# Joining the two maps of differential attention ahead of the transposes, and issuing the first tile's output projection within the last attention steps

## The chip, the cores and the metric

One core of a Trainium2 chip runs the whole program. The metric is device time in microseconds (us) of one execution; lower is better. Five engines work side by side and meet through semaphores: TensorE (PE, matmuls), VectorE (DVE), ScalarE (ACT), GpSimd (POOL) and SyncE (SP), which issues the weight loads. Each engine takes its own instructions strictly in the order of the program.

## The reference

Two transformer layers over 256 tokens of width 1024, all in float32. Layer 0: swiglu, post-norm, a sparse attention (NSA), post-norm, swiglu, post-norm; its result also gives shared keys and values. Layer 1: swiglu, post-norm, differential attention, post-norm, swiglu, post-norm. The change is in the differential attention, eight heads with two maps each:

```python
lam = exp(sum(lq1 * lk1)) - exp(sum(lq2 * lk2)) + lambda_init
a = attn_map(q1b, k1) - lam * attn_map(q2b, k2)      # causal softmax maps, head dim 64
o = einsum('bhqk,bkhe->bqhe', a, v)                  # value dim 128
o = rms_norm(o, subln_g) * (1.0 - lambda_init)
return o.reshape(B, S, D_MODEL) @ w_out
```

## The kernel before, in words

**Weights.** A weight matrix passes in units of 128x2048 values through four slots of `raw`, `w_hi` and `w_lo`. SP loads a unit once the unit four before it is split. Splitting means: ACT copies `raw` to a rounded `w_hi` (L575), DVE subtracts for `w_lo` (L781); in the attentions POOL does both in quarters (L502, L503). A product is then three matmuls, hi by hi, hi by lo and lo by hi (`three`, L1193 to L1195). `unit_used` frees a slot when PE has finished a unit for token tile 1. Tokens go in two tiles of 128. Each stage (`STAGES`) fills `acc` banks 0 and 1 for tile 0, then 2 and 3 for tile 1; a norm of DVE (L822 to L835) reads them, with a root by POOL (L480, L481), and its gain and bias come by a DMA of POOL (`load_norm`, L475) into `norm_gb`, whose space the probabilities share until the last of them is transposed.

**Differential queries.** Stage `diff_q` has four units. While PE runs tile 1 of it, it also transposes the rotated keys (L1252) and swaps their halves (L1438); ACT copies the even parts of four (L589), DVE the odd ones (L814), from two banks of `trb` in turn. Each turned part needs the part two before it to be copied. DVE evicts the queries (L1102), POOL rotates them (L488 to L491), ACT and DVE split them (`split_beside`, L603, L808), and PE turns them, those of tile 0 before the loop, those of tile 1 within its steps 2 to 5 (`LATE_PARTS`).

**The loop.** `DIFF_JOBS` has 12 jobs: tile 0 has four jobs of two heads (maps of 128 keys), tile 1 eight jobs of one head (maps of 256 keys). A job fills one bank of 512 columns. `DIFF_TURNS` groups them: turn 0 is jobs 0 and 1, turn 1 jobs 2 and 3, turn 2 jobs 4 to 7, turn 3 jobs 8 to 11; a turn fills one 512-wide output per map. `job_steps` gives 15 steps. At step i, each engine in its own order:
- PE: scores of job i (L1375, and the mask L1377) into the bank i modulo 3 of three, after the exponentials of job i-3; transposes of the four probability blocks of job i-2; late query parts; value products of job i-3 (L1396), map 0 into `acc[:, 2]`, map 1 into `acc[:, 3]`.
- ACT: copy of the turned blocks of job i-2 (L589), late query parts, exponentials of job i, with their row sums (L664).
- DVE: negated maximum of job i (L930); the pieces of a finished turn: `diff_read` (L1134 to L1138: reciprocals of the sums, times lambda, both outputs scaled out of PSUM), one step later `diff_subtract` (L1151 to L1154: difference, square, reduce, scale and epsilon), then POOL's power -1/2 (L557) and `diff_norm` (L1161, L1162).
- At steps 10 and 11 (`TILE0_DONE`) PE turns the two halves of the finished tile 0 (`("x", "diff_o", 0)`), ACT and DVE write their high and low parts (L583, L791).
- POOL, beside the loop, splits units 0 and 1 of the output projection, then the powers, with unit 2 after the second; the norm's gain and bias are loaded after the third power. Unit 3 is split by ACT and DVE behind the loop.

**The projection.** `out_stage` waits for the last exponential, runs the four units for tile 0 (16 products of three matmuls), with the turns of tile 1 ahead of its last unit (`turn_o`, waits for the last norm), then tile 1. DVE's norm of tile 0 starts when `tile0_full` says so (L822); behind it DVE splits the first units of the next swiglu, `ffn3`.

## Time and profile before

| what | us |
|---|---|
| runs of the kernel: median, lowest, highest of 3 | 1071.84, 1071.44, 1075.18 |
| the profiled execution, its own time | 1070.39 |
| its span, first to last instruction | 1068.3 |
| PE, DVE, ACT, POOL busy in the span | 1033.2, 596.3, 460.7, 125.1 |
| mean granted clock of TensorE | 0.997 |

The durations below are of the one profiled execution, its times counted from the start of its span. A granted clock of 1.00 is TensorE's full 2.4 GHz. Successive instructions of an engine overlap a little, so that the distance from start to start is shorter than the duration shown; where work is summed up, that distance counts.

### The profile page before, as it was taken

The page shows a single profiled execution, that of the slowest core. Times are in us where ns is not written, and L with a number is a line of the kernel's source. Part 1 is how long each engine was busy: PE and PEld are TensorE (multiplying, and loading weights), DVE is VectorE, ACT ScalarE, POOL GpSimd, SP SyncE. Part 2 cuts the span into 40 slices and gives each one's busy share as a digit, 9 for nine tenths or more (in the row PEclk, how much of TensorE's full clock was granted, in tenths as well). Part 3 has the DMA queues.
Part 4 walks back from the last instruction along what each step waited for, and adds up shares of the span by engine and source line. Part 5 has one row for each costly group of instructions (what it writes and reads, how often), then busy time and mean ns, then how long its engine had stood idle before and what let it go on. Part 6 is the DMA issues. An engine that isn't in the chain of part 4 may idle for free.

```text
span 1068.3 us, 13273 instructions
## 1 busy us (share of the span) xinstructions
PE 1033.2 (97%) x5334; PEld 868.8 (81%) x5334; DVE 596.3 (56%) x543; ACT 460.7 (43%) x568; POOL 125.1 (12%) x157
## 2 busy tenths in 40 slices
PE   7999999999999999999999999999997899999997
PEld 6888888889898788898878888888876778888885
DVE  4455543854755754462575544554666884455444
ACT  4555432333773454452434334433436444454430
POOL 1000000232911100000012000000017510000001
...
DMA packets 78652, 178.51 MB, mean 167 GB/s; under 512 B 2992, under 2 KB 12352, under 8 KB 78608
## 3 DMA queue, kind: packets, MB, share of 16 engines
...
q14 instruction: 11, 0.09, 0.0%
...
## 4 chain that ended last, share of the span: by engine, by line
PE 82%; DVE 13%; POOL 3%; ACT 1%; DMA 1%; issue 1%; SPq 0%; POOLq 0%; DVEq 0%; ACTq 0%
PE acc L1193 24%; PE acc L1195 24%; PE acc L1194 24%; DVE w_lo L781 4%; PE trb L1252 4%; PE acc L1396 2%; POOL rstd L480 1%; DVE stats L827 1%; DVE x L835 1%; DVE y L822 1%; PE acc L1375 1%; DMA raw<-ffn_w_gate 1%; DVE neg_max L930 1%; DVE xt_lo L791 1%; PE aux L1445 1%
## 5 line engine op out<-in xcount | busy, mean ns | idle before, releaser
L781 DVE TENSOR_TENSOR w_lo<-raw,w_hi 128x2048 fp32r<-128x2048 f32 (+1 forms) x153 | 348.7, 2283 | 217.4 <-ACT w_hi L575 217.4
L575 ACT ACTIVATE w_hi<-raw 128x2048 fp32r<-128x2048 f32 (+1 forms) x153 | 291.7, 1908 | 259.0 <-PE acc L1195 252.1
L1193 PE MATMUL acc<-w_hi,xt_hi 128*128 128x512 f32 (+1 forms) x992 | 378.8, 382 | 6.0 <-DVE w_lo L781 4.6
L1195 PE MATMUL acc<-w_hi,xt_lo 128*128 128x512 f32 (+1 forms) x992 | 371.9, 375 | 0.0
L1194 PE MATMUL acc<-w_lo,xt_hi 128*128 128x512 f32 (+1 forms) x992 | 371.4, 374 | 0.0
L1193 PEld LDWEIGHTS acc<-w_hi,xt_hi 128*128 128x128 f32 x992 | 186.9, 188 | 41.0 <-DVE w_lo L781 6.5
L1195 PEld LDWEIGHTS acc<-w_hi,xt_lo 128*128 128x128 f32 x992 | 186.7, 188 | 34.2
L1194 PEld LDWEIGHTS acc<-w_lo,xt_hi 128*128 128x128 f32 x992 | 187.1, 189 | 31.4
L1193 PE MATMUL acc<-w_hi,ht_hi 128*128 128x512 f32 x352 | 139.4, 396 | 0.0
L1195 PE MATMUL acc<-w_hi,ht_lo 128*128 128x512 f32 x352 | 138.9, 395 | 0.0
L1194 PE MATMUL acc<-w_lo,ht_hi 128*128 128x512 f32 x352 | 138.9, 395 | 0.0
L480 POOL TENSOR_SCALAR rstd<-mean_var 128x1 f32<-128x1 f32 x12 | 15.2, 1268 | 796.0 <-DVE mean_var L829 787.9
L1195 PEld LDWEIGHTS acc<-w_hi,ht_lo 128*128 128x128 f32 x352 | 66.3, 188 | 15.5
L1193 PEld LDWEIGHTS acc<-w_hi,ht_hi 128*128 128x128 f32 x352 | 66.3, 188 | 15.0
L1194 PEld LDWEIGHTS acc<-w_lo,ht_hi 128*128 128x128 f32 x352 | 66.3, 188 | 15.0
L619 ACT ACTIVATE ht_hi<-trb 128x512 f32 (+2 forms) x48 | 26.7, 556 | 109.1 <-PE trb L1252 109.1
L851 DVE TENSOR_TENSOR ht_lo<-trb,ht_hi 128x512 f32 (+2 forms) x48 | 30.5, 642 | 72.7 <-ACT ht_hi L619 72.7
L615 ACT ACTIVATE y<-acc 128x512 f32<-128x512 f32 (+1 forms) x48 | 27.0, 563 | 73.3 <-PE acc L1195 73.3
L846 DVE SCALAR_TENSOR_TENSOR y<-y,acc 128x512 f32<-128x512 f32 (+1 forms) x48 | 30.7, 639 | 45.4 <-ACT y L615 45.4
L583 ACT ACTIVATE xt_hi<-trb 128x512 fp32r<-128x512 f32 x32 | 17.7, 596 | 64.4 <-PE trb L1252 64.4
L503 POOL TENSOR_TENSOR w_lo<-raw,w_hi 128x512 fp32r<-128x512 f32 x28 | 37.8, 1349 | 2.2
L1252 PE MATMUL trb<-id_r,y 128*128 128x128 f32 x200 | 30.5, 272 | 3.8 <-POOL y L525 1.7
...
## 6 DMA issues: line engine op xcount, KB each, us to landing
...
```

What stands on the lines that cost most here:

```text
L480: link(pool.tensor_scalar(rstd[:, tok, 0:1], mean_var[:, tok, 1:2], EPS, None, ALU.add))
L503: ins = pool.tensor_tensor(w_lo[:, slot, part], raw[:, slot, part], hi.bitcast(F32), ALU.subtract)
L575: act.activation(w_hi[:, slot, 0:k * c], raw[:, slot, 0:k * c], ACT.Copy).then_inc(hi_ready, 1)
L615: act.activation(sil[:, tok, 0:c], acc[:, 2 * tok, 0:c], ACT.Silu).then_inc(silu_done, 1)
L619: act.activation(ht_hi[:, bass.ds(4 * g, k), tok * P:(tok + 1) * P], trb[:, bank, 0:k * P].rearrange("p (k c) -> p k c", c=P), ACT.Copy).t ...
L781: dve.tensor_tensor(w_lo[:, slot, 0:k * c], raw[:, slot, 0:k * c], w_hi[:, slot, 0:k * c].bitcast(F32), ALU.subtract).then_inc(lo_ready, 1)
L846: dve.scalar_tensor_tensor(h_nat[:, tok, 0:c], sil[:, tok, 0:c], 0.5, acc[:, 2 * tok + 1, 0:c], ALU.mult, ALU.mult).then_inc(acc_free, 1)
L851: dve.tensor_tensor(ht_lo[:, bass.ds(4 * g, k), tok * P:(tok + 1) * P], trb[:, bank, 0:k * P].rearrange("p (k c) -> p k c", c=P), ht_hi[:, ...
L1193: pe.matmul(out_ap, s_hi, hi, start=first, stop=False)
L1194: pe.matmul(out_ap, s_hi, lo, start=False, stop=False)
L1195: return pe.matmul(out_ap, s_lo, hi, start=False, stop=last)
L1252: ins = pe.transpose(trb[:, bank, j * P:(j + 1) * P], b, ident)
```

## The change

- **Order of a job.** When a job's exponentials are done, DVE joins its two maps in SBUF (`join_maps`): a reciprocal of the second sums, a small product with the first sums and minus lambda, and for each head one `scalar_tensor_tensor` over the map (first + share * second). PE then transposes two blocks in place of four and multiplies two in place of four; the output of a turn lies in one bank, turns alternating between `acc[:, 2]` and `acc[:, 3]`. The division by the first sum is left out, and the norm's epsilon is scaled by the sum's square instead.
- **Norm.** The squares with their sums go to ACT, from PSUM (`squares_of`), two small operations to DVE (`diff_sums`), the power stays with POOL, and `diff_norm` reads PSUM in four pieces; it runs at fixed steps 6, 8 and 12. `diff_read` and `diff_subtract` go. Turn 2 and 3 wait, before their first product, for the norm that read their bank.
- **Order on the engines.** ACT runs the exponentials of a step before its copies. DVE copies the first two late query parts, and splits the last queries in step 0, behind the first maximum. The last key copy goes ahead of the eviction of the second queries.
- **Projection.** Tile 0 of it is cut into eight pieces of six matmuls (`diff_out_piece`), issued in steps 10 (one), 11 (one), 12 (two), 13 (one), two behind the loop, one behind the turn of tile 1. Since they use `acc` banks 0 and 1, scores 9 to 11 use the two `aux` banks (`diff_bank`). Halves of tile 0 are turned at steps 7 and 9.
- **Splits and loads.** Units 0 and 1 of the projection are split by ACT and DVE between the key copies, units 2 and 3 by POOL from step 0 on, unit 3 in halves between the powers. `load_norm(4)` comes after the fourth power.

The diff, cut to its core:

```diff
 
-TILE0_DONE = {"nsa": (14, 15), "diff": (10, 11)}
+TILE0_DONE = {"nsa": (14, 15), "diff": (7, 9)}
+
+DIFF_NORM_STEP = {0: 6, 1: 8, 2: 12}
+
+DIFF_OUT_STEPS = {10: (0,), 11: (1,), 12: (2, 3), 13: (4,)}
 
 LATE_PARTS = {"nsa": {6: (0,), 9: (1,), 11: (2,), 13: (3,)}, "diff": {2: (0,), 3: (2,), 4: (1,), 5: (3,)}}
...
         score_bank = [acc[:, 0], acc[:, 1], aux[:, 0]]
+        diff_bank = [score_bank[i % 3] for i in range(9)] + [aux[:, 1], aux[:, 0], aux[:, 1]]
...
-            split_units(UNIT_OF["diff_out"], UNIT_OF["diff_out"] + 2)
-            for k in range(len(DIFF_TURNS)):
+            n = UNIT_OF["diff_out"] + 2
+
+            def diff_root(k):
                 pool.wait_ge(rms_ready, k + 1)
-                pool.tensor_tensor(rms[:, 1, k, :], rms[:, 0, k, :], half_pow[:], ALU.pow).then_inc(rms_pow, 1)
-                if k == 1:
-                    split_units(UNIT_OF["diff_out"] + 2, UNIT_OF["diff_out"] + 3)
-                if k == len(DIFF_TURNS) - 2:
-                    load_norm(4)
+                pool.tensor_tensor(rms[:, 2, k, :], rms[:, 1, k, :], half_pow[:], ALU.pow).then_inc(rms_pow, 1)
+
+            pool.wait_ge(beside_ready, 8)
+            pool.wait_ge(lo_ready, n)
+            split_unit(n)
+            diff_root(0)
+            split_unit(n + 1, range(2))
+            diff_root(1)
+            split_unit(n + 1, range(2, 4))
+            diff_root(2)
+            diff_root(3)
+            load_norm(4)
...
+
+            def copy_joined(j):
+                t = TURN_OF["p", "diff", j]
+                act.wait_ge(tr_full, t + 1)
+                act.activation(turned_probs[:, j % 2, 0:2 * P], trb[:, t % 2, 0:2 * P], ACT.Copy).then_inc(
+                    tr_free[t % 2], 1)
+
+            def squares_of(turn):
+
+                act.wait_ge(turn_full, len(NSA_TURNS) + turn + 1)
+                for k in range(4):
+                    ins = act.activation(branch[0][:, k * DIFF_V:(k + 1) * DIFF_V],
+                                         acc[:, 2 + turn % 2, k * DIFF_V:(k + 1) * DIFF_V], ACT.Square,
+                                         accum_out=rms[:, 0, turn, k:k + 1])
+                ins.then_inc(squares_summed, 1)
+
+            def split_parts(n, parts):
+
+                slot, (k, c) = n % SLOTS, unit_shape(n)
+                act.wait_ge(raw_in[slot], 16 * (n // SLOTS + 1))
+                act.wait_ge(unit_used, n - SLOTS + 1)
+                for q in parts:
+                    part = slice(q * k * c // 4, (q + 1) * k * c // 4)
+                    ins = act.activation(w_hi[:, slot, part], raw[:, slot, part], ACT.Copy)
+                if q == 3:
+                    ins.then_inc(hi_ready, 1)
 
...
             act.activation(lam[:, 0:2], lam[:, 0:2], ACT.Exp).then_inc(lam_exp, 1)
+            split_units(n0 + 4, n0 + 5)
 
             for part in (0, 2):
                 copy_heads(("kr", "diff"), 0, part, dks[:, 0])
...
+                split_parts(n0 + 5, (part, part + 1))
             for tok in range(TOKS):
                 for part in (0, 2):
...
-                if tr:
-                    copy_p("diff", i - 2)
-                for part in LATE_PARTS["diff"].get(i, ()):
-                    copy_heads(("qr", "diff"), 1, part, dqs)
                 if sc:
                     exps("diff", DIFF_JOBS, i, len(NSA_JOBS))
+                if tr:
+                    copy_joined(i - 2)
+                if i > 3:
+                    for part in LATE_PARTS["diff"].get(i, ()):
+                        copy_heads(("qr", "diff"), 1, part, dqs)
+                if pv >= 0 and DIFF_JOBS[pv][3]:
+                    squares_of(DIFF_JOBS[pv][0])
                 if i in TILE0_DONE["diff"]:
                     x_high("diff_o", 0, [TILE0_DONE["diff"].index(i)])
-            act.wait_ge(lo_ready, n0 + 7)
-            split_units(n0 + 7, n0 + 8)
             x_high("diff_o", 1)
...
+            split_parts(n0 + 4, (0, 1))
+            copy_heads("kr", 0, 1, dks[:, 0])
+            split_parts(n0 + 4, (2, 3))
+            copy_heads("kr", 0, 3, dks[:, 0])
             split_beside(6)
-            for part in (1, 3):
-                copy_heads("kr", 1, part, dks[:, 0])
-            for part in (1, 3):
-                copy_heads("ks", 0, part, dks[:, 1])
+            copy_heads("kr", 1, 1, dks[:, 0])
+            copy_heads("kr", 1, 3, dks[:, 0])
+            split_parts(n0 + 5, (0,))
+            copy_heads("ks", 0, 1, dks[:, 1])
+            split_parts(n0 + 5, (1,))
+            copy_heads("ks", 0, 3, dks[:, 1])
             copy_heads("ks", 1, 1, dks[:, 1])
+            copy_heads("ks", 1, 3, dks[:, 1])
             diff_queries_out(1)
-            copy_heads("ks", 1, 3, dks[:, 1])
             for part in (1, 3):
                 copy_heads("qr", 0, part, dqs)
-            split_beside(7)
-
-            def diff_read(turn):
+            split_parts(n0 + 5, (2, 3))
...
+            def join_maps(i):
+
+                _, tok, heads, _ = DIFF_JOBS[i]
+                width = P * (tok + 1)
+                hs = slice(heads[0], heads[-1] + 1)
+                dve.wait_ge(exp_done, len(NSA_JOBS) + i + 1)
+                link(dve.reciprocal(share[:, 1, hs], sums[:, tok, 1, hs]))
+                link(dve.scalar_tensor_tensor(share[:, 0, hs], sums[:, tok, 0, hs], lam[:, 3:4], share[:, 1, hs],
+                                              ALU.mult, ALU.mult))
+                for k, h in enumerate(heads):
+                    first = probs[:, i % 3, 2 * k * width:(2 * k + 1) * width]
+                    second = probs[:, i % 3][:, (2 * k + 1) * width:(2 * k + 2) * width]
+                    ins = dve.scalar_tensor_tensor(first, second, share[:, 0, h:h + 1], first, ALU.mult, ALU.add)
+                ins.then_inc(maps_joined, 1)
...
+                first_sums = sums[:, tok, 0, 4 * g:4 * g + 4]
+                link(dve.scalar_tensor_tensor(rms[:, 1, turn, :], first_sums, EPS, first_sums, ALU.mult, ALU.mult))
+                dve.wait_ge(squares_summed, turn + 1)
+                dve.scalar_tensor_tensor(rms[:, 1, turn, :], rms[:, 0, turn, :], 1.0 / DIFF_V, rms[:, 1, turn, :],
+                                         ALU.mult, ALU.add).then_inc(rms_ready, 1)
...
+                o, to = acc[:, 2 + turn % 2], dq[:, tok, g * 512:(g + 1) * 512]
                 dve.wait_ge(rms_pow, turn + 1)
...
+                for k in range(4):
+                    at = slice(k * DIFF_V, (k + 1) * DIFF_V)
+                    ins = dve.scalar_tensor_tensor(to[:, at], o[:, at], rms[:, 2, turn, k:k + 1], sub_g[:], ALU.mult,
+                                                   ALU.mult)
+                ins.then_inc(turn_mixed, 1)
+
             for i, sc, tr, pv in job_steps(DIFF_JOBS):
                 if sc:
-                    maxima(DIFF_JOBS, i, len(NSA_JOBS))
-                for turn in range(last):
-                    if ends_turn(DIFF_JOBS, pv - 1, turn):
-                        diff_subtract(turn)
-                    if turn < 2 and ends_turn(DIFF_JOBS, pv - norm_lag[turn], turn):
+                    maxima(DIFF_JOBS, i, len(NSA_JOBS), diff_bank[i])
+                if i == 0:
+                    split_beside(7)
+                if i and i - 1 < len(DIFF_JOBS):
+                    join_maps(i - 1)
+                if i <= 3:
+                    for part in LATE_PARTS["diff"].get(i, ()):
+                        copy_heads("qr", 1, part, dqs)
+                for turn in range(len(DIFF_TURNS) - 1):
+                    if i == DIFF_NORM_STEP[turn]:
                         diff_norm(turn)
                 if pv >= 0 and DIFF_JOBS[pv][3]:
-                    diff_read(DIFF_JOBS[pv][0])
+                    diff_sums(DIFF_JOBS[pv][0])
                 if i in TILE0_DONE["diff"]:
                     x_low("diff_o", 0, [TILE0_DONE["diff"].index(i)])
-            diff_subtract(last)
-            diff_norm(last - 1)
-            diff_norm(last)
-            split_units(n0 + 7, n0 + 8)
+            diff_norm(len(DIFF_TURNS) - 1)
             x_low("diff_o", 1)
             out_stage("diff_out")
             ffn_stage("ffn3", lambda: x_low("diff_out", 1))
...
+                    pe.wait_ge(acc_free, e + 1)
+                elif DIFF_JOBS[j - 1][3] and turn_no >= 2:
+                    pe.wait_ge(turn_mixed, len(NSA_TURNS) + turn_no - 1)
...
+                    for kb in range(tok + 1):
+                        ins = pe.matmul(acc[:, 2 + turn_no % 2, (h % 4) * DIFF_V:(h % 4 + 1) * DIFF_V],
+                                        turned_probs[:, j % 2, k * P:(k + 1) * P],
+                                        v_b[:, kb, h * DIFF_V:(h + 1) * DIFF_V], start=(kb == 0), stop=(kb == tok))
+                        k += 1
+                if last:
+                    ins.then_inc(turn_full, 1)
+
+            def diff_out_piece(kt):
+
+                n = UNIT_OF["diff_out"] + kt // 2
+                if kt == 0:
+                    pe.wait_ge(exp_done, len(NSA_JOBS) + 8)
+                if kt % 4 == 0:
+                    copied("x", "diff_o", 0, kt // 4)
+                pe.wait_ge(lo_ready, n + 1)
+                for c in range(2):
+                    cols = slice(c * 512, (c + 1) * 512)
+                    ins = three(acc[:, c], xt_hi[:, kt, 0:P], xt_lo[:, kt, 0:P], weights(w_hi, n)[:, kt % 2, cols],
+                                weights(w_lo, n)[:, kt % 2, cols], kt == 0, kt == KT - 1)
+                if kt == KT - 1:
+                    finish(0, ins)
...
+                    pe.wait_ge(acc_free, e)
                     for tok, part in parts:
                         copied("ks", "diff", tok, part)
                 if sc:
-                    scores(DIFF_JOBS, i, base, lambda h, m: dqs[:, 8 * m + h],
+                    if i >= 3:
+                        pe.wait_ge(exp_done, len(NSA_JOBS) + i - 1 - (i < 10))
+                    scores(DIFF_JOBS, i, diff_bank[i], lambda h, m: dqs[:, 8 * m + h],
                            lambda h, m, part: dks[:, part, 8 * m + h])
+                for kt in DIFF_OUT_STEPS.get(i, ()):
+                    diff_out_piece(kt)
                 if tr:
-                    turn_p("diff", i - 2, base)
+                    pe.wait_ge(maps_joined, i - 1)
+                    _, tok, heads, _ = DIFF_JOBS[i - 2]
+                    turn(("p", "diff", i - 2), [probs[:, (i - 2) % 3, j * P:(j + 1) * P]
+                                                for j in ((0, 1) if tok else (0, 2))])
                 for part in LATE_PARTS["diff"].get(i, ()):
                     turn_heads(("qr", "diff"), 1, part, 7)
                 if pv >= 0:
-                    values("diff", DIFF_JOBS, pv,
-                           lambda h, m, kb: v_b[:, kb, h * DIFF_V:(h + 1) * DIFF_V], DIFF_V, diff_first, 4)
+                    diff_values(pv)
                 if i in TILE0_DONE["diff"]:
                     half = TILE0_DONE["diff"].index(i)
                     pe.wait_ge(turn_mixed, len(NSA_TURNS) + half + 1)
                     turn_wide(("x", "diff_o", 0), dq[:, 0, :], [half])
-            out_stage("diff_out", "diff_o")
+            for kt in (5, 6):
+                diff_out_piece(kt)
+            pe.wait_ge(turn_mixed, len(NSA_TURNS) + len(DIFF_TURNS))
+            turn_wide(("x", "diff_o", 1), dq[:, 1, :])
+            diff_out_piece(7)
+            group(1, FILL_OF["diff_out", 0, 1], UNIT_OF["diff_out"], range(4), rows_unit(xt_hi, xt_lo, KT),
+                  {3: lambda: turn_x("diff_out", 0)}, ("x", "diff_o", 1))
             ffn_stage("ffn3", lambda: turn_x("diff_out", 1), ("x", "diff_out"), False)
```

## Rows read from the trace of the kernel before

**Rows 1.** Page: chain that ended last, shares by engine; two costly groups of instructions.
```profile
PE 82%; DVE 13%; POOL 3%; ACT 1%; DMA 1%; issue 1%; SPq 0%; POOLq 0%; DVEq 0%; ACTq 0%
...
L781 DVE TENSOR_TENSOR w_lo<-raw,w_hi 128x2048 fp32r<-128x2048 f32 (+1 forms) x153 | 348.7, 2283 | 217.4 <-ACT w_hi L575 217.4
L575 ACT ACTIVATE w_hi<-raw 128x2048 fp32r<-128x2048 f32 (+1 forms) x153 | 291.7, 1908 | 259.0 <-PE acc L1195 252.1
```
**Rows 2.** Table by stage: length; PE, PEld, DVE, ACT, POOL busy (count); clock, DMA, GB/s.
```profile
788.60:803.20 14.60, 14.60 (x78) 11.13 (x77) 5.97 (x8) 5.73 (x9) 1.96 (x4) 1.00 0.00 1
817.20:843.20 26.00, 20.10 (x172) 18.62 (x172) 24.40 (x39) 16.10 (x53) 18.23 (x18) 1.00 0.27 86
842.00:843.00 1.00, 0.00 (x0) 0.00 (x0) 0.96 (x3) 0.00 (x0) 0.37 (x1) 1.00 0.82 121
843.20:846.70 3.50, 3.41 (x20) 3.44 (x21) 0.28 (x2) 2.40 (x2) 1.63 (x3) 0.62 0.87 331
```
**Rows 3.** Timeline of PE: start us, duration us, line, operation, count, [idle before <- releaser].
```profile
805.35 1.06 PE L1252 MATMUL trb<-id_r,y 128*128 128x128 f32 x8 [1.57 <-DVE dks L814]
...
807.40 0.41 PE L1375 MATMUL acc<-dks,dqs 128*128 128x128 f32 x2
...
830.89 0.48 PE L1375 MATMUL acc<-dks,dqs 128*128 128x256 f32 x2
...
831.65 0.61 PE L1252 MATMUL trb<-id_r,norm_gb 128*128 128x128 f32 x4
832.09 1.06 PE L1396 MATMUL acc<-v_b,y 128*128 128x128 f32 x8
832.91 0.48 PE L1375 MATMUL acc<-dks,dqs 128*128 128x256 f32 x2
```
**Rows 4.** Timeline of DVE, same columns, 784 to 862 us.
```profile
784.09 0.28 DVE L1094 TENSOR_TENSOR y<-lam_in 128x128 f32<-128x128 f32 x1
...
784.61 2.35 DVE L808 TENSOR_TENSOR dqs<-k_nat,dqs 128x1024 fp32r<-128x1024 f32 x2
...
808.40 1.88 DVE L808 TENSOR_TENSOR xt_lo<-k_nat,xt_lo 128x1024 fp32r<-128x1024 f32 x1 [0.19 <-ACT xt_lo L603]
...
819.04 0.98 DVE L1135 TENSOR_SCALAR share<-share,lam 128x4 f32<-128x4 f32 x1
...
821.27 0.68 DVE L930 TENSOR_REDUCE neg_max<-aux 128x2 f32<-128x512 f32 x1
821.87 1.15 DVE L1151 TENSOR_TENSOR k_nat<-k_nat,y 128x512 f32<-128x512 f32 x1
...
829.14 0.69 DVE L1152 TENSOR_TENSOR y<-k_nat 128x512 f32<-128x512 f32 x1
...
839.99 1.65 DVE L1152 TENSOR_TENSOR y<-k_nat 128x512 f32<-128x512 f32 x1
...
843.29 0.23 DVE L1135 TENSOR_SCALAR share<-share,lam 128x4 f32<-128x4 f32 x1
...
859.17 1.22 DVE L822 SCALAR_TENSOR_TENSOR y<-x,acc 128x1024 f32<-128x1024 f32 x1 [1.25 <-PE acc L1195]
...
861.99 1.28 DVE L832 SCALAR_TENSOR_TENSOR y<-y,mean_var,norm_gb 128x1024 f32<-128x1024 f32 x1
```
**Rows 5.** Timeline of POOL in the attention, same columns.
```profile
818.73 1.27 POOL L503 TENSOR_TENSOR w_lo<-raw,w_hi 128x512 fp32r<-128x512 f32 x1
...
825.71 1.03 POOL L557 TENSOR_TENSOR rms<-rms,half_pow 128x4 f32<-128x4 f32 x1 [1.55 <-DVE rms L1154]
...
844.49 0.66 POOL L475 DMA_DIRECT2D norm_gb<-norm_gain  x1 [0.85 <-PE trb L1252]
```
**Rows 6.** Timeline of ACT: one exponential of a first-tile job.
```profile
811.27 0.36 ACT L664 ACTIVATE norm_gb<-acc,neg_max 128x128 f32<-128x128 f32 x1
```
**Rows 7.** Chain of waits, one product of the output projection (start us, us).
```profile
854.84 0.23 PE acc L1193
```
**Rows 8.** DMA issues, 840 to 866 us: KB each, median us to landing.
```profile
norm_gb<-norm_bias POOLq DMA_DIRECT2D x1, 512.0 KB, 4.7
```

123 lines of the change are left out of this document (54 added, 69 removed).

## The prediction

> **What bounds the kernel now.** I read the chain that ended last first: TensorE (PE) holds 82% of it and VectorE (DVE) 13% [rows 1]. The weight products that fill most of the span are not touched, so the question is which stretch of DVE the change reaches. The table by stage answers: from 817.2 to 843.2 us, inside the differential attention, DVE is busy 24.4 of 26.0 us and PE 20.1 of 26.0; in the stretch before it, 788.6 to 803.2, PE is full and DVE and ScalarE (ACT) are busy 6.0 and 5.7 of 14.6 us [rows 2]. Then the order of PE: it idles 1.57 us at 805.35 for a key copy on DVE, starts the scores of step 0 at 807.40 and those of step 10 at 832.91 [rows 3]; the queue of VectorE takes up the first projected tile (L822) at 859.17 [rows 4]. From there on the two kernels do the same work, and DVE is again what the chain runs through, so the price of the change is the shift of that 859.17. Three pieces: up to step 0, steps 0 to 9, and step 10 to the end of tile 0.
>
> **The lock.** DVE's operations with all operands in SBUF wait for a running GpSimd (POOL) operation: the 128x4 tensor_scalar takes 0.98 us at 819.04 and 0.23 at 843.29; a 128x512 tensor_tensor takes 1.15 and 1.65 beside POOL, 0.69 without (829.14); the 128x1024 one 1.88 beside it and 1.2 (2.35 for two) without [rows 4]. POOL's operation that ran at 819.04 had started at 818.73 and took 1.27 [rows 5]: DVE resumed when it ended. Over the 11 such operations that began while POOL split weights (the first at 808.40, the last at 839.99), the excess adds to 5.1 us, 0.45 each. Maxima, copies and norms that read PSUM show no excess. The change gives DVE many small operations of the waiting kind.
>
> **Piece 1, up to step 0: minus 1.5 us, then 0.5 back.** The last key copy now precedes the 1.2 us eviction of the queries, so the 1.57 us idle ahead of the second query turn goes [rows 3]; scores 0 start near 805.9. The splits of output units 0 and 1 leave POOL: twice 1.9 us more on ACT, one and a half times 2.2 us (2.28 less the overlap) more on DVE [rows 1], inside 788.6 to 803.2, where each has over 8 us idle [rows 2]; hidden, and if they were not, PE's turns of the keys would be late by what sticks out. The second half of unit 1 (1.1 us) lies on DVE's path, at 806.6, and meets POOL's rotation: 0.5 us more, which delays the rotated queries and so the first exponentials. POOL starts unit 2 only after the query split of step 0, which so takes 1.2 us in place of 1.88 [rows 4].
>
> **Piece 2, steps 0 to 9.** Removed from DVE for a turn: two scaled reads, subtract, square, reduce, two norm operations, some 5.2 us without waits (seven 512-wide passes at 0.6 to 0.7 and three small ones). Added: a join for every job. Its two 128x256 or 128x128 halves are nearest to the 0.28 us of a 128x128 tensor_tensor [rows 4]; pipelined, with 1.07 ns an element from there to 0.69 at 512, 0.2 each for two heads or 0.37 for one. With the reciprocal (0.22) and the small product of sums (0.26, nearest to the 0.23 of the tensor_scalar), a join is 0.86 us. PE needs, before scores 10, the norm of turn 1 in DVE's step 8. DVE's account from 806.6 to there: 9 maxima at 0.60 (821.27 to 821.87 [rows 4]) 5.4; 8 joins 6.9; half unit 1.1; query split 1.2; two late copies 1.2; two norms of four 128-wide pieces (0.2 each as above, and the hand-over) 1.7; two sets of small sums 0.9; one low part 0.6: 19.0, with hand-overs 19.6. POOL splits units 2 and 3 beside it, so joins 0, 1, 2 (three waiting operations each) and 4 to 7 (two each), plus one small sum, wait: 18 x 0.45 = 8.1, and 0.5 from piece 1. Waits on others: the squares of turn 0 hold DVE 2.4 us, since ACT must first finish the exponentials and copies of that step and then four squares, priced as the 0.36 of a 128-wide exponential [rows 6], 1.4 in all; the high part of the turned tile holds it 0.5. Behind the waiting instruction stands the next step's maximum, for which ACT waits, then the join, then PE's turn. 19.6 + 8.6 + 2.9 = 31.1: DVE is through at 837.7, and scores 10 start at 837.9 where they stood at 832.91: **5.0 us later**. PE loses half its transposes and value products here (four transposes 0.44, 831.65 to 832.09, and values 0.82, to 832.91, per job [rows 3]; 0.63 us a job saved) but it is not the one that is late. In front of scores 4, for example, stand three joins and two copies, where ACT copied before.
>
> **Piece 3, from scores 10 to L822 of tile 0.** Before: 859.17 - 832.91 = 26.3. Now PE has work throughout: two score groups at 0.76 (830.89 to 831.65 [rows 3]) 1.5; seven pieces of the projection, each 6 products at 0.23 [rows 7], 9.7; four turns at 0.22 0.9; five value groups at 0.41 2.0: 14.1, so 852.0. DVE and ACT keep up (join 11 is due some 2 us before PE wants it). The last turn's values end two pieces (2.8) earlier, at 849.2; squares 1.4, small sums 0.45, POOL's power 1.03 [rows 5], norm 0.85 and hand-overs 0.3 make 853.2: PE idles 1.2 there. Eight transposes 0.9, piece seven 1.4, hand-over 0.2: 855.7. **17.8 in place of 26.3, minus 8.5.** Unit 3's split and DVE's 2.2 us for it leave this stretch; they were off the path. The load of the norm's gain moves behind the last power: issued near 852.1, it takes 0.66 to issue [rows 5] and 4.7 to land [rows 8], so 857.5; L832 wants it 2.8 us after L822 (859.17 to 861.99 [rows 4]), 858.5. It is hidden with 1 us to spare; beyond that each microsecond would be lost in full. The tighter ring of two banks for scores 10 and 11 waits for exponentials that are over: nothing.
>
> **Sum:** 5.0 - 8.5 = **-3.5 us**. The profiled execution is 1070.39 (span 1068.3 and 2.1 around it), so 1066.9 there; the median of the runs is 1.45 above it, so 1068.3.
>
> Bounds: the lock costs from 0 (joins that fall between POOL's operations; sum -11.6, 1060.2) to a whole 1.27 us operation [rows 5] for most of the 18 (up to 23, +11). I take 0.45, the mean of the same kind of operation beside the same POOL work. The joins themselves may be 0.1 to 0.3 off each, 1 to 3 us.
> The rows show a 128x1024 scalar_tensor_tensor with two SBUF tensors at 1.28 us (861.99) beside 1.2 for a tensor_tensor of that size [rows 4]: no halved rate.
> The Trainium skill, Vector Engine (DVE) Microarchitecture Reference, Points that are easy to get wrong, says such an operation with two sources that are not bf16 runs at half throughput; the twelve joins would then cost about 3 us more by an estimate from its factor, the sum -0.5 and the time 1071.3; the row of this case speaks against it, and it gets no chance of its own.
>
> **Rivals.**
> *Lock cheap (0.25).* The joins meet POOL half as often: the pattern maximum, reciprocal, join gives POOL's operation 0.8 us to end. For: the reciprocal and the maximum take no lock. Against: after each join the waiting POOL operation starts at once. Price: 4 of the 8.1 us back, 1064.3.
> *The clock (0.15).* TensorE was granted 1.00 at 842 to 843, where it did nothing, and 0.62 on the mean of the next stretch, 843.2 to 846.7 [rows 2], its level of 1.2 GHz in place of 2.4 for three quarters of it: of 2.7 us at half speed 1.3 are lost, or 1.5 with the edge. The new loop leaves PE idle some 3 us at step 2 and 2 to 3 us at steps 4 and 8, with less work between. Two such falls where PE is next late cost 3.0: 1071.3. Against: from 817.2 to 843.2, with 5.9 us of idle, the clock was 1.00 throughout [rows 2].
> The Trainium skill, TensorE: Matmul & The Clock Gate, HAM oscillation, warns of just this, idle gaps that bring back the low clock each time; the row from 843.2 agrees, the stretch before it does not.
> *Slower (0.08).* Place: between stt and join, and between the two joins of a job, where a POOL operation that queued meanwhile goes first. Then the 18 operations wait 0.95 us each, 9 more: 1077.3. It decides against the change from 0.64 us a wait (3.5/18 + 0.45). Against: the trace's mean of 0.45.
> *It doesn't do what it says (0.07).* The pieces are issued in steps 10 to 13, but PE has no idle time to fill there and pushes maxima 11 and join 11 back; the last norm comes later by as much: about no change, 1071.8.
> *Forecast (0.45):* 1066 to 1070.5.
>
> **Numbers.** What a measurement of this kernel can tell from no change is about 0.5%, 5.4 us. Faster by more: the lock rival (0.25) and a fifth of the forecast (0.09), 0.34. Slower by more: 0.08 and a little of the clock, 0.09. The rest 0.57. The range reaches down over most of the cheap lock (1062) and up over the clock and no change (1074.5); it leaves out the slow rival and the extreme of the cheap one.
>
> **What would show it.** Right: scores 0 near 806; scores 10 near 838; joins of 0.25 to 0.4 us alone and 0.8 to 1.5 beside POOL; PE full from step 10 until one idle of about 1 us before the last turn; L822 at 855 to 856; no table load before the squares. Wrong: scores 10 before 834 (lock overpriced) or after 841 (underpriced); granted clock 0.5 in the loop more than once; L832 idle on the gain's load; DVE not the releaser of PE's waits in steps 2 to 9.

## The result and the profile after

| kernel | runs | median, us | lowest to highest, us | ratio to the kernel before, 95% interval |
|---|---|---|---|---|
| before, beside it | 8 | 1073.98 | 1071.22 to 1075.56 | |
| changed | 8 | 1064.88 | 1063.88 to 1069.02 | 0.9933 [0.9914, 0.9952] |
| changed, once more (e0_after) | 12 | 1068.05 | 1063.75 to 1069.81 | 0.9951 [0.9934, 0.9968] |

The ratios weigh all runs, and so differ from the ratios of the two medians (which are 9.1 and 3.3 us apart); in the second comparison the kernel before has a median of 1071.36 us. The change makes the kernel faster, by 0.67% (7.2 us, from 5.2 to 9.2) in the first comparison and by 0.49% (5.3 us, from 3.4 to 7.1) in the second. The forecast was 3.5 us and a time of 1068.3. The range held; the forecast size was half to two thirds of what came. The likeliest verdict, no difference beyond 0.5%, lies at the edge of the first interval and in the middle of the second. The profiled execution took 1065.26 us (span 1063.3, granted clock 0.992), beside 1070.39 and 1068.3 of before.

The page has the same chain: PE first, then DVE, whose small share fell by a point [rows 1].

```profile
PE 81%; DVE 12%; POOL 2%; ACT 2%; issue 1%; DMA 1%; SPq 0%; POOLq 0%; DVEq 0%; ACTq 0%
```

Table by stage, columns as in [rows 2]: the key stage, scores 0 to scores 10, scores 10 to the norm of tile 0, then three pieces of the loop.

```profile
788.00:802.50 14.50, 14.02 (x74) 10.25 (x73) 9.65 (x15) 9.28 (x14) 1.73 (x4) 1.00 0.22 73
805.90:836.60 30.70, 21.98 (x153) 19.60 (x153) 26.03 (x57) 17.54 (x79) 18.95 (x21) 0.83 0.23 74
836.60:854.90 18.30, 17.23 (x99) 13.94 (x97) 9.05 (x30) 8.39 (x36) 3.15 (x4) 1.00 0.27 86
...
811.00:815.00 4.00, 2.20 (x11) 2.20 (x11) 3.93 (x7) 2.68 (x16) 3.84 (x5) 0.52 0.41 158
815.00:819.00 4.00, 3.40 (x19) 2.99 (x18) 3.93 (x8) 1.92 (x10) 2.74 (x3) 0.63 0.03 4
819.00:823.00 4.00, 3.31 (x26) 2.85 (x27) 1.76 (x7) 2.15 (x11) 0.00 (x0) 1.00 0.77 259
```

The splits of output units 0 and 1 fit beside the keys, but not for nothing: PE is busy 14.0 of 14.5 us there, where it was busy all of the time before. In the loop DVE is busy 26.0 of 30.7 us, and from scores 10 on PE 17.2 of 18.3. The clock is 0.52 from 811 to 815; PE's idle time of step 2 ends in that stretch, at 812.80.

Timeline of PE, columns as in [rows 3].

```profile
790.59 0.63 PE L1313 MATMUL trb<-id_r,dqs 128*128 128x128 f32 x4 [0.36 <-ACT dks L608]
...
804.51 0.63 PE L1313 MATMUL trb<-id_r,y 128*128 128x128 f32 x4 [0.34 <-ACT dqs L608]
...
805.88 0.41 PE L1431 MATMUL acc<-dks,dqs 128*128 128x128 f32 x2
...
812.80 0.69 PE L1313 MATMUL trb<-id_r,norm_gb 128*128 128x128 f32 x2 [3.15 <-DVE norm_gb L1204]
...
835.16 0.44 PE L1313 MATMUL trb<-id_r,norm_gb 128*128 128x128 f32 x2 [1.69 <-DVE norm_gb L1204]
...
836.61 0.48 PE L1431 MATMUL aux<-dks,dqs 128*128 128x256 f32 x2
...
852.38 1.09 PE L1313 MATMUL trb<-id_r,k_nat 128*128 128x128 f32 x8 [1.01 <-DVE k_nat L1223]
```

Scores 0 start at 805.88 where they started at 807.40, the 1.57 us wait for a key copy [rows 3] is now 0.34, scores 10 start at 836.61 (832.91 before), and the one idle time between them and the last turn is 1.01 us, ahead of that turn. The wait at 790.59 is new: PE's turn of the keys waits for a key copy of ACT, which now stands behind ACT's split of unit 0 (1.92 us from 788.04 on).

Timeline of DVE, columns as in [rows 4].

```profile
808.70 1.23 DVE L857 TENSOR_TENSOR xt_lo<-k_nat,xt_lo 128x1024 fp32r<-128x1024 f32 x1
...
810.89 1.86 DVE L1204 SCALAR_TENSOR_TENSOR norm_gb<-norm_gb,share 128x128 f32<-128x128 f32 x2
...
823.78 0.17 DVE L1213 SCALAR_TENSOR_TENSOR rms<-rms 128x4 f32<-128x4 f32 x1 [1.91 <-ACT y L704]
...
826.10 1.14 DVE L1199 SCALAR_TENSOR_TENSOR share<-sums,lam,share 128x1 f32<-128x1 f32 x1
827.27 0.78 DVE L1204 SCALAR_TENSOR_TENSOR norm_gb<-norm_gb,share 128x256 f32<-128x256 f32 x1
827.98 1.11 DVE L1223 SCALAR_TENSOR_TENSOR k_nat<-acc,rms,sub_g 128x128 f32<-128x128 f32 x4
...
836.84 0.22 DVE L1199 SCALAR_TENSOR_TENSOR share<-sums,lam,share 128x1 f32<-128x1 f32 x1
837.10 0.48 DVE L1204 SCALAR_TENSOR_TENSOR norm_gb<-norm_gb,share 128x256 f32<-128x256 f32 x1
...
854.91 1.22 DVE L871 SCALAR_TENSOR_TENSOR y<-x,acc 128x1024 f32<-128x1024 f32 x1
...
857.73 1.29 DVE L881 SCALAR_TENSOR_TENSOR y<-y,mean_var,norm_gb 128x1024 f32<-128x1024 f32 x1
```

Read the pairs: the small product of sums takes 0.22 us alone (836.84) and 1.14 beside POOL (826.10); a 128x256 join 0.48 alone and 0.78 beside it. L871 is the old L822: 854.91 in place of 859.17 [rows 4], and L881 follows with no wait for the norm's gain.

**Where the rest came from.** L871 is 4.26 us earlier, but it also had a head start: the last norm ahead of the attention, at 777.12 before, is at 776.29 here, 0.83 us earlier. VectorE aggregates one norm per token tile, so its BATCH_NORM_AGGREGATE starts cut the trace into segments that can be laid beside each other.

```profile
861.75 0.21 DVE L829 BATCH_NORM_AGGREGATE mean_var<-stats 128x2 f32<-128x12 f32 x1
...
875.71 0.21 DVE L829 BATCH_NORM_AGGREGATE mean_var<-stats 128x2 f32<-128x12 f32 x1
...
1052.07 0.21 DVE L829 BATCH_NORM_AGGREGATE mean_var<-stats 128x2 f32<-128x12 f32 x1
```

These are three of the kernel before (tile 0 and tile 1 behind the differential attention, tile 0 behind the last swiglu); of the changed kernel the same three:

```profile
857.49 0.21 DVE L878 BATCH_NORM_AGGREGATE mean_var<-stats 128x2 f32<-128x12 f32 x1
...
871.78 0.21 DVE L878 BATCH_NORM_AGGREGATE mean_var<-stats 128x2 f32<-128x12 f32 x1
...
1047.38 0.21 DVE L878 BATCH_NORM_AGGREGATE mean_var<-stats 128x2 f32<-128x12 f32 x1
```

From 875.71 to 1052.07 are 176.36 us, from 871.78 to 1047.38 175.60. The segments in the same way (those left out differ by 0.03 us or less, the end behind the last norm by 0.1):

| segment, by its ends | before, us | changed, us | difference |
|---|---|---|---|
| start to tile 0 of the first swiglu's norm | 191.92 | 191.06 | -0.86 |
| tile 1 there to the first maximum of the sparse attention | 55.89 | 57.45 | +1.56 |
| second swiglu; shared keys and values with the third swiglu | 176.34, 219.86 | 175.60, 219.11 | -0.74, -0.75 |
| last norm ahead of the attention to its first maximum | 33.08 | 31.76 | -1.32 |
| first maximum to tile 0's norm | 51.55 | 49.44 | -2.11 |
| tile 0's to tile 1's norm | 13.96 | 14.29 | +0.33 |
| fourth swiglu, and the last norm | 176.36, 10.04 | 175.60, 9.87 | -0.76, -0.17 |

The differential attention gave 3.43 us up to tile 0 and took back 0.33; all four swiglus, whose code the change does not touch, gave 0.74 to 0.86 each, 3.11 in all. Against that stands a loss of 1.56 us in front of the sparse attention, which is a matter of the execution and not of the change. The table by stage has for that stretch, in the kernel before, the changed one, and the changed one in e0_after:

```profile
205.50:261.30 55.80, 53.47 (x328) 46.96 (x327) 31.08 (x52) 18.55 (x26) 16.55 (x32) 1.00 0.43 149
```
```profile
204.60:262.00 57.40, 55.07 (x328) 48.14 (x327) 31.13 (x53) 18.55 (x26) 16.52 (x32) 0.97 0.42 146
```
```profile
204.60:265.30 60.70, 58.37 (x328) 51.04 (x327) 30.74 (x54) 18.55 (x26) 16.48 (x32) 0.92 0.40 139
```

One and the same program, the changed kernel, needs 57.4 or 60.7 us for it, at a granted clock of 0.97 or 0.92. That is 3.3 of the 3.7 us between these two executions (1065.26 and 1068.96). Single executions of one kernel lie up to 6 us apart, so from here on segments of traces are compared beside the medians.

What the swiglus gained shows in one row of the view of one tile's matmuls (duration in ns, lowest, median and highest), before and changed:

```profile
L1194 PE MATMUL acc<-w_lo,ht_hi x352: 390/393/404, 139.0 to 1060.0; 128*128 128x512 f32 x176
```
```profile
L1255 PE MATMUL acc<-w_lo,ht_hi x352: 387/392/398, 138.8 to 1055.1; 128*128 128x512 f32 x176
```

The products of the second half of a swiglu, whose stationary tiles are `ht_hi` and `ht_lo`, are a little shorter. There are three times 352 of them, and 3.11 us over 1056 is 2.9 ns each. The change made the tile `rms` larger by 64 bytes a partition, and every tile behind it in SBUF moved up by that.

### The profile page after: what moved, and what is told of

Its sections match the earlier page's. It is cut to its first block, busy times and chain, and to the rows that moved or that the text cites. A ratio compares the mean times of both kernels' runs of the same rounds, so it can differ in the third digit from the quotient of the medians.

```text
span 1063.3 us, 13191 instructions
## 1 busy us (share of the span) xinstructions
PE 1027.4 (97%) x5262; PEld 863.4 (81%) x5262; DVE 596.2 (56%) x577; ACT 463.4 (44%) x602; POOL 115.5 (11%) x149
## 4 chain that ended last, share of the span: by engine, by line
PE 81%; DVE 12%; POOL 2%; ACT 2%; issue 1%; DMA 1%; SPq 0%; POOLq 0%; DVEq 0%; ACTq 0%
PE acc L1254 24%; PE acc L1256 24%; PE acc L1255 24%; DVE w_lo L830 4%; PE trb L1313 4%; PE acc L1452 2%; DMA raw<-ffn_w_up 1%; POOL rstd L487 1%; DVE stats L876 1%; DVE x L884 1%; DVE y L871 1%; PE acc L1431 1%; DVE neg_max L979 1%; ACT w_hi L594 1%; DVE xt_lo L840 1%
## 5 line engine op out<-in xcount | busy, mean ns | idle before, releaser
L895 DVE SCALAR_TENSOR_TENSOR y<-y,acc 128x512 f32<-128x512 f32 (+1 forms) x48 | 30.7, 639 | 45.3 <-ACT y L634 45.3
L509 POOL TENSOR_TENSOR w_lo<-raw,w_hi 128x512 fp32r<-128x512 f32 x24 | 31.3, 1304 | 1.9
```

The source lines that it names most:

```text
L509: ins = pool.tensor_tensor(w_lo[:, slot, part], raw[:, slot, part], hi.bitcast(F32), ALU.subtract)
L895: dve.scalar_tensor_tensor(h_nat[:, tok, 0:c], sil[:, tok, 0:c], 0.5, acc[:, 2 * tok + 1, 0:c], ALU.mult, ALU.mult).then_inc(acc_free, 1)
```

## The experiments

All kernels were timed against the kernel before on the same chip, in three groups (e0 to e3; e4 to e7; e8 to e11), in which the kernel before had medians of 1071.36, 1071.79 and 1072.04 us. "Loop" below is the distance from the first maximum (DVE) to the norm of tile 0 (L871): 48.97 us before (859.17 - 810.20), 46.86 in the changed kernel (854.91 - 808.05). Each is one execution. Two more traces of the loop of before, e5 and e11, have 49.41 and 48.53; e0_after has 47.27. A difference below 1 us between two loops therefore says nothing.

**e0_after, the changed kernel again.**

> The changed kernel itself, run beside the next three as their yardstick. If the shift of the first projected tile (854.91 against 859.17 us) is the whole effect, its time stands 4 to 5 us under the kernel before when both show the same granted clock, and what its median gains beyond that comes with a difference of clock between the runs. Rival: something else in the change is worth 2 to 4 us more, and then the gain is 7 us or more at equal clock too.

Measured: above, ratio 0.9951. The lowest times lie 6.3 us apart (1063.75 and 1070.02), though the changed kernel's clock is the lower one (0.994 and 0.996): more than the 4 to 5 us of the first theory, less than the rival's 7.

**e1_nosplit, POOL without the splits of units 2 and 3** (their products then use what lies in the slot).

```diff
             def split_unit(n, quarters=range(4)):
+                if n >= UNIT_OF["diff_out"]:
+                    pool.wait_ge(raw_in[slot], 16 * (n // SLOTS + 1))
+                    pool.wait_ge(unit_used, n - SLOTS + 1)
+                    ...
+                    return
```

> Left out: POOL's splitting of output units 2 and 3 (their high and low parts are whatever the slots held; the signals stay). Theory of the lock: the operations of the joins that took 1.86, 2.00, 1.14, 1.30 and 0.51 us beside POOL fall to 0.2 to 0.6; summed over the loop the excess is 5.5 us, and as DVE is the bound of steps 0 to 9, scores 10 start 4 to 5.5 us earlier (near 832) and the time falls by 4 to 5.5 us. Rival: DVE is not the bound there (ACT and PE are), the waits vanish and scores 10 start at most 1.5 us earlier, the time falls by under 1.5 us.

Measured: 1061.51 us (1058.84 to 1066.0), ratio 0.9895 [0.987, 0.9921]. The joins, timeline of DVE:

```profile
812.31 0.22 DVE L1207 SCALAR_TENSOR_TENSOR share<-sums,lam,share 128x2 f32<-128x2 f32 x1
812.56 0.61 DVE L1212 SCALAR_TENSOR_TENSOR norm_gb<-norm_gb,share 128x128 f32<-128x128 f32 x2
...
824.23 0.16 DVE L1221 SCALAR_TENSOR_TENSOR rms<-rms 128x4 f32<-128x4 f32 x1 [1.90 <-ACT y L712]
```

Two joins take 0.61 us where they took 1.86: the lock is the cause of the excess. In the changed kernel's trace it adds up to 5.8 us (1.25 at 810.89, 1.39 at 814.00, 0.92 at 826.10, 1.08 at 833.28, 1.2 in five smaller ones). In the profiled execution scores 10 start 26.42 us after the first maximum (836.14 - 809.72), 2.1 earlier than in the changed kernel (28.56), and the loop became only 1.7 us shorter (45.17), since DVE then waits for scores that PE computes at a low clock (1.44 us at 816.94), and still 1.90 for ACT's squares; scores 10 are computed at a low clock too. The lowest times differ by 4.9 us and the medians by 6.5, but not at the same clock: the lowest execution here had a mean clock of 0.999. At 0.994 the two kernels have 1062.06 and 1063.75, 1.7 us apart again. So the lock is worth 1.7 us at equal clock, near the rival's 1.5, and up to some 5 us where the clock stays up as well, as the theory had it.

**e2_behind, all pieces of tile 0's projection behind the loop.**

```diff
-DIFF_OUT_STEPS = {10: (0,), 11: (1,), 12: (2, 3), 13: (4,)}
+DIFF_OUT_STEPS = {}
...
-            for kt in (5, 6):
+            for kt in range(7):
                 diff_out_piece(kt)
```

> The eight pieces of tile 0's projection issued behind the loop (seven ahead of the turn of tile 1, one behind it); all else as changed. Theory: five pieces are 6.8 us of PE that steps 10 to 13 cover only in part, since those steps are now bound by DVE and ACT at some 2.3 us each: values of job 11 end 3 to 4 us earlier, the seven pieces then take 9.6 us, the last norm is hidden, and L871 of tile 0 comes 2 to 4 us later than 854.9; time +2 to +4 us. Rival: overlap is worth nothing since PE had no idle there: under +1 us. Other rival: the overlap is the whole gain of the change: +5 us or more.

Measured: 1070.53 us, ratio 0.9984 [0.9968, 1.0], 0.0033 above e0_after. PE's timeline shows what the pieces had filled:

```profile
842.88 0.69 PE L1313 MATMUL trb<-id_r,norm_gb 128*128 128x128 f32 x2 [1.98 <-DVE norm_gb L1204]
...
855.88 1.04 PE L1313 MATMUL trb<-id_r,k_nat 128*128 128x128 f32 x8
```

The loop is 51.87 us (858.36 - 806.49), 5.0 more than with the overlap and 2.9 more than in the kernel before. The joins without the overlap, then, lengthen the loop; that the time is still not above that of before comes from the shorter swiglus and the earlier key copy, which this kernel keeps.

**e3_keycopy, the last key copy behind the eviction again.**

```diff
+            diff_queries_out(1)
             copy_heads("ks", 1, 3, dks[:, 1])
-            diff_queries_out(1)
```

> Undone alone: the last key copy goes behind the eviction of the second queries again. By the sum of the prediction the scores of step 0 return from 805.9 to 807.4 and the time rises by 1.5 us. Rival: the loop does not start with the scores but with ACT, whose first exponential waits at 808.76 for the split of the rotated queries; then the first maximum moves from 808.05 to at most 808.7 and the time rises by 0.7 us or less.

Measured: 1069.24 us (lowest 1066.73), ratio 0.9974 [0.996, 0.9987], 0.0023 above e0_after. The old wait is back:

```profile
803.65 1.06 PE L1313 MATMUL trb<-id_r,y 128*128 128x128 f32 x8 [1.57 <-DVE dks L863]
```

The segment up to the first maximum is 33.02 us, as in the kernel before (33.08), in place of 31.76: the order of this one copy is 1.26 of the 1.32 us of that segment. Scores 0 start 31.10 us after the last norm here (805.71 - 774.61), 29.59 in the changed kernel (805.88 - 776.29) and 30.28 in the kernel before (807.40 - 777.12). So the copy gives 1.5 us at scores 0, as forecast, and the rest of the change costs 0.8 there: PE's turns of the keys are 0.8 us late from 792.03 on, behind two waits, the larger the one at 790.59. The loop grew too, by 1.9 us to 48.79, with scores 10 at half clock.

**e4_filler, 88 small matmuls in PE's idle time of steps 2, 6, 7 and 9.**

```diff
+                for _ in range({2: 36, 6: 20, 7: 8, 9: 24}.get(i, 0)):
+                    pe.matmul((acc[:, 0] if i == 9 else aux[:, 1])[:, 0:P], id_bf[:], id_bf[:], start=True, stop=True)
```

> The changed kernel with 88 small bf16 matmuls (128x128, into banks that hold nothing then) where PE stood idle in steps 2, 6, 7 and 9, so that the low clock of 812 to 818 and 828 to 831 us should not come. Theory of the prediction's account (DVE is what is late there): the clock is at its high level through the loop and the time falls by under 1 us. Rival of the clock: both falls were on the path and 1.5 to 3 us come back.

Measured: 1064.4 us (1063.51 to 1067.39), ratio 0.9928 [0.9907, 0.9949]. Table by stage:

```profile
811.00:815.00 4.00, 2.91 (x45) 2.74 (x45) 3.93 (x8) 2.39 (x14) 3.22 (x4) 1.00 0.74 254
815.00:819.00 4.00, 2.51 (x23) 2.17 (x22) 3.90 (x8) 1.92 (x10) 3.84 (x5) 1.00 0.00 0
819.00:823.00 4.00, 2.63 (x15) 2.28 (x14) 2.26 (x5) 1.64 (x9) 0.45 (x1) 0.64 0.62 179
```

The low clock left 811 to 819 and came at 820 instead. The lowest time, 1063.51, belongs to an execution with a mean clock of 0.999, that is with hardly any fall, and it is 0.24 us below the lowest of the changed kernel (1063.75, clock 0.994). The loop of the profiled execution is 47.32 us, no shorter than in the changed kernel. So taking the early falls away is worth nothing that can be measured, as the theory had it; what the fillers themselves cost is not known. It says nothing of a fall that comes later, over scores 10: see e6.

**e5_shift, the kernel before with 64 bytes more in front of the late tiles, and nothing else.**

```diff
-        rms = sb("rms", [P, 2, 4, 4])
+        rms = sb("rms", [P, 3, 4, 4])
```

> The kernel before with one edit: the tile rms is declared [P, 3, 4, 4] in place of [P, 2, 4, 4], so that k_nat, v_b, ht_hi, ht_lo and the attention tiles lie 64 bytes higher in each partition; no instruction changes. In every kernel with the change the four down-projections of the swiglu stages run at 2.75 us a unit where the kernel before needs 2.80. Theory of the placement: this comes from where the transposed hidden rows (the stationary operand) lie, so this kernel shows 2.75 too, 0.75 us less a stage and 3 us less in all (ratio near 0.997). Rival: it comes from another part of the change, such as the program's length or the loads' timing: 2.80 stays and the time is that of before.

Measured: 1067.81 us, ratio 0.9956 [0.9942, 0.997]. The swiglus have the segments of the changed kernel (191.07, and 175.59 for the second), and the row of `ht_hi` its numbers:

```profile
L1194 PE MATMUL acc<-w_lo,ht_hi x352: 387/392/398, 138.9 to 1058.6; 128*128 128x512 f32 x176
```

**e6_noshift, the changed kernel without the 64 bytes** (the powers go into unused columns of `share`).

```diff
-        rms = sb("rms", [P, 3, 4, 4])
+        rms = sb("rms", [P, 2, 4, 4])
+        roots = [share[:, k // 2, 8 + 4 * (k % 2):12 + 4 * (k % 2)] for k in range(4)]
```

> The changed kernel with rms at its old size, the roots kept in unused columns of share: nothing behind rms moves. Theory of the placement: the down-projections return to 2.80 us a unit and the time is 3 us above the changed kernel's at the same granted clock; what is left against the kernel before is the gain of the attention stage alone, some 3.4 to 4 us. Rival: nothing changes against the changed kernel.

Measured: 1068.92 us (lowest 1068.03), ratio 0.9982 [0.9966, 0.9998]. The swiglus are back at 191.98 and 176.32 us.

```profile
L1256 PE MATMUL acc<-w_lo,ht_hi x352: 390/393/404, 139.0 to 1060.4; 128*128 128x512 f32 x176
```

This is the change as its text describes it: 0.2% (1.9 us, from 0.2 to 3.6). The forecast of 3.5 lies just inside. The profiled execution (1070.55 us) has the 31.76 us up to the first maximum, but a loop of 48.83 (859.35 - 810.52), 0.14 less than before. The clock had fallen over scores 10, where it had not in e0_after, with PE busy throughout in both:

```profile
839.80:842.50 2.70, 2.70 (x11) 2.32 (x11) 1.66 (x4) 1.65 (x6) 0.00 (x0) 0.51 0.93 347
```
```profile
840.20:842.90 2.70, 2.70 (x20) 2.31 (x18) 1.63 (x6) 1.78 (x6) 0.00 (x0) 1.00 0.97 364
```

From scores 10 to the norm of tile 0 are 19.49 us here and 18.30 in e0_after, with the same instructions but for the place of the powers: a fall there costs 1.2 us. e1, e2, e3 and e8 show one there too, each in its one profiled execution.

**e7_overlap, the kernel before with the overlap alone.** The old joins stay, `diff_out_piece` is issued in steps 12 to 14, `diff_bank` is used, and unit 3 is split ahead of the last norms.

```diff
...
+                for kt in {12: (0,), 13: (1, 2), 14: (3,)}.get(i, ()):
+                    diff_out_piece(kt)
...
-            out_stage("diff_out", "diff_o")
+            for kt in (4, 5, 6):
+                diff_out_piece(kt)
+            pe.wait_ge(turn_mixed, len(NSA_TURNS) + len(DIFF_TURNS))
+            turn_wide(("x", "diff_o", 1), dq[:, 1, :])
+            diff_out_piece(7)
```

> The kernel before with the overlap alone: pieces 0 to 3 of tile 0's projection in steps 12 to 14, 4 to 6 behind the loop, the turn of tile 1, piece 7; scores 9 to 11 in the aux banks; DVE splits unit 3 ahead of the last subtraction. Joins, norm and the rest as before. Theory: what the overlap can give is bound by the last norm, whose chain here is the old one (two reads 1.3, subtract to epsilon 2.2, split 2.2, power 1.0, norm 1.4 us behind the last product): the turn of tile 1 starts near 857 and L822 of tile 0 stays within 1 us of 859.2; time within 1 us of before. Rival: the overlap alone gives the 4 us or more, joined maps or not.

Measured: 1075.05 us, ratio 1.0026 [1.001, 1.0041]: slower than the kernel before. The loop is 52.24 us (863.58 - 811.34).

```profile
859.70 1.97 PE L1255 MATMUL trb<-id_r,k_nat 128*128 128x128 f32 x8 [3.54 <-DVE k_nat L1165]
```

PE waits 3.54 us for the last norm: the products of tile 0 had covered the old, long norm chain, and now they are done ahead of it. But this kernel also puts unit 3's split into that chain, between the reads of the last turn and its subtraction (timeline of DVE):

```profile
852.17 2.28 DVE L783 TENSOR_TENSOR w_lo<-raw,w_hi 128x2048 fp32r<-128x2048 f32 x1
```

It holds the chain for 2.20 us (to 854.37), so by an estimate 1.3 of the 3.54 us, and a loop of some 50.0, would be left without it. The overlap with the old joins and the split elsewhere was not tried. Taken with e2: the joins without the overlap make the loop 2.9 us longer, the overlap in this form 3.3, both together make it 2.1 shorter. The pieces fill the idle time that the joins leave. That the short norm chain lets them move ahead, more than the place of the split, is likely and not shown.

**e8_latesums, the small sums of a turn one step later.**

```diff
-                if pv >= 0 and DIFF_JOBS[pv][3]:
-                    diff_sums(DIFF_JOBS[pv][0])
+                if pv >= 1 and DIFF_JOBS[pv - 1][3]:
+                    diff_sums(DIFF_JOBS[pv - 1][0])
...
+            diff_sums(len(DIFF_TURNS) - 1)
```

> The changed kernel with the small sums of a turn (and so the wait for ScalarE's squares) one step later, behind the next maximum and join. My theory: VectorE's waits of 1.91 us (turn 0) and 1.55 us (turn 2) stand in front of the next maximum on a queue that sets scores 10, so both go. But each norm now has its power later: turn 1's norm (step 8) must still have it. Expected: no wait over 0.5 us ahead of the sums of turns 0 to 2, scores 10 some 1 to 2 us earlier after the first maximum (28.6 us before), time 1 to 2 us below the changed kernel, 1063. Rival: the waits are filled by nothing because the norms wait in their place (for POOL's power): scores 10 no earlier than 0.5 us, time within 0.7 us of the changed kernel's 1064 to 1065.

Measured: 1066.67 us (lowest 1064.28), ratio 0.9953 [0.9936, 0.997]: nothing gained. The waits did go, but look at the same windows of the table by stage:

```profile
815.00:819.00 4.00, 3.38 (x15) 2.53 (x14) 3.92 (x8) 1.84 (x10) 2.64 (x3) 0.50 0.12 8
819.00:823.00 4.00, 3.91 (x18) 3.67 (x18) 1.60 (x5) 1.58 (x6) 0.00 (x0) 0.50 0.74 254
```

PE is at half clock to 823, where the changed kernel had 1.00 from 819 on; its scores now come late, and DVE's maximum at 823.95 waits 1.58 us for them. Scores 10 start 28.98 us after the first maximum (836.93 - 807.95), no earlier than in the changed kernel (28.56), and the loop is 49.02 us, 2.2 longer.

**e9_early, one piece a step from step 9.**

```diff
-DIFF_OUT_STEPS = {10: (0,), 11: (1,), 12: (2, 3), 13: (4,)}
+DIFF_OUT_STEPS = {9: (0,), 10: (1,), 11: (2,), 12: (3,), 13: (4,)}
```

> The changed kernel with its pieces of the projection spread one to a step from step 9 to 13 (one in 9, 10, 11, 12, 13 in place of one in 10, one in 11, two in 12, one in 13). My theory: PE waits for VectorE in step 9, so a piece (1.38 us) put there runs in time that is idle, and everything from step 12 on comes up to 1.4 us earlier; but the idle time ahead of the last turn, 1.01 us, then grows unless the last values also come earlier. Expected: L871 (the norm's first operation for tile 0) 0.7 to 1.4 us earlier after the first maximum than 46.9 us, time about 1 us lower. Rival: PE reaches scores 10 later by the piece, since it waits less there than the trace shows: no change within 0.5 us, or up to 1 us slower.

Measured: 1064.81 us, ratio 0.9933 [0.9908, 0.9959]. The piece did fill idle time, 1.69 us ahead of the turn at 835.16 became 0.50, and the loop is 46.66 us, 0.2 shorter: the gain is within what can't be told.

**e10_both, e8 and e9 together.**

> Both edits of the two kernels before together (sums one step later; pieces one to a step from step 9). My theory: the idle time of PE is where the piece of step 9 goes only if VectorE does not come earlier; with the waits for the squares gone PE's idle shrinks, so the two gains overlap: 1.5 to 2.5 us in all, 1062 to 1063. Rival: they add fully or cancel: 3 us or more, or nothing.

Measured: 1062.36 us (1061.01 to 1067.3), ratio 0.9906 [0.9882, 0.993], the fastest kernel of the study that computes all of it. The loop is 45.45 us (857.00 - 811.55), 1.4 less than in the changed kernel, with PE full from 843:

```profile
843.00:847.00 4.00, 4.00 (x25) 3.39 (x25) 3.04 (x12) 3.52 (x18) 0.94 (x1) 1.00 0.51 195
```

Each edit alone did nothing that can be told, both gave 2.7 us by the lowest times; the interval lies below that of e0_after, but overlaps that of the first comparison (from 0.9914). The trace suggests why both are needed: in e8 the clock was low a second time, over scores 10; here 819 to 827 is the only stretch at 0.50, and nothing takes the shorter DVE queue's gain back. That was read from one execution each and not tested further.

**e11_shift128, the kernel before with 128 bytes more.**

```diff
-        rms = sb("rms", [P, 2, 4, 4])
+        rms = sb("rms", [P, 4, 4, 4])
```

> The kernel before with 128 bytes more a partition in front of the late tensors (rms [P,4,4,4] in place of [P,2,4,4]; nothing else differs). 64 bytes more gave -4 us, in all four feed-forward stages' second products (their stationary operand ht_hi, ht_lo moved; 2.75 in place of 2.80 us a unit). If what counts is the position modulo 128 bytes, the stages keep the old pitch here: BATCH_NORM segments as in the kernel before within 0.2 us, time within 1.5 us of it. If any other position than the old one helps, each of the four stages is 0.7 us shorter, as with 64 bytes, and the time about 3 to 4 us lower.

Measured: 1067.79 us (lowest 1064.53), ratio 0.9955 [0.9936, 0.9975]. The first swiglu's norm is at 190.64, 1.28 us earlier than before where 64 bytes gave 0.85, and the next two segments are 175.22 and 218.70.

```profile
L1194 PE MATMUL acc<-w_lo,ht_hi x352: 387/389/398, 138.8 to 1054.5; 128*128 128x512 f32 x176
```

So it is not the position modulo 128 bytes, and other positions than the old one do not all help alike: three positions have three medians in this row, 393, 392 and 389 ns. The last is that of the products with `xt_hi` (389, over mixed widths), a tile ahead of which every tile has a multiple of 8192 bytes. Why the position matters was not tried further, nor was e10 with these 128 bytes.

## Why the prediction was right and wrong

**Piece 1, the copy right, the splits wrong, the number luck.** Forecast 1.5 us less, scores 0 at 805.9; measured 805.88. The copy gave its 1.5 (e3). But the splits beside the keys, costed as hidden, made PE's turns of the keys 0.8 us late, which the prediction had named as what would happen if they were not. The clock time came out right since the whole attention began 0.83 us early; counted from the norm ahead of it, scores 0 came only 0.7 us earlier. The split before the first maximum stuck out by 0.26 (1.54 at 806.58 in place of 1.28), where 0.5 was allowed.

**Piece 2, right in sum, wrong in its parts.** Scores 10 were forecast 5.0 us later, at 837.9, and came at 836.61, which is 4.5 later when the head start is taken off. The lock was priced at 8.6 (18 operations by 0.45, and 0.5) and cost 5.8; only eight rows of the loop met POOL, some for up to 1.4 us. Long waits on few, where the forecast had short ones on all. POOL's gaps explain it: its powers wait for DVE's sums, so its splits bunch at 810 to 818, 825 to 829 and 830 to 835, and in between the joins are free. The squares took 0.25 from start to start in place of 0.36, and the wait for them 1.91 in place of 2.4. What PE waited for in steps 2 to 9 was DVE, as forecast, but for 1.9 us of waits for ACT. A join without POOL took, from start to start, 0.41 for 128x256 and 0.53 for two of 128x128, where 0.37 and 0.4 were forecast. The duration of 0.48 for 128x256 lies between the 0.28 and 0.69 of tensor_tensors of 128 and 512 columns [rows 4], within 0.06 of the line through them: no halved rate.
The Trainium skill, Vector Engine (DVE) Microarchitecture Reference, Points that are easy to get wrong, has half throughput for such an operation; the measurement decides against it here.

**Piece 3, right.** Forecast 17.8 us from scores 10 to the norm, measured 18.30 (836.61 to 854.91) in this execution and in e0_after, 19.49 in e6; forecast idle 1.2 us, measured 1.01. L871 was forecast at 855.7. The norm's gain was issued at 851.12 and was there in time.

**What failed: "From there on the two kernels do the same work, and DVE is again what the chain runs through, so the price of the change is the shift of that 859.17".** They do the same work, but not at the same speed: the 3.11 us of the swiglus were outside the sum. A grown tile in the diff, `rms` from 2 to 3 rows, was read as bookkeeping. e5 gives the placement alone 0.44%, e6 the change without it 0.18%, and the two add up to 0.62%, between the 0.49 and 0.67% of both.

The sum over the attention, 5.0 - 8.5 = -3.5, came as 4.53 - 7.96 = -3.43 in the profiled execution (and +0.33 behind it). That closeness is in part luck: from the norm ahead of the attention to L871 e0_after shows -3.03 and e6, with the clock low over scores 10, -1.46, and in e6's time 3.5 is the far end of the interval (0.2 to 3.6).

**The rivals.** *Lock cheap* (4 of 8.1 us back) had 2.5 of them right, and its 1064.3 was near the result, but for a wrong reason in the main. *The clock*: two falls came, at step 2 and ahead of scores 8 (0.52 from 811, 0.57 from 828.05 to 832.05, mean 0.83 from scores 0 to scores 10), which the prediction had as a sign of being wrong. In e4, whose fillers keep the clock up at step 2, the time was the same, since DVE was the late one. The rival was right for neighbours: in e6, e8 and e3 a fall lies over scores 10, where PE has work throughout, and in e6 it costs 1.2 us from there to the norm. *Slower* from 0.64 us a wait: the mean over the 18 is 0.31 (5.6 us in the loop). *It doesn't do what it says*: PE was full from step 10, so no.
